# Differential attention: the join one tile later on VectorE, its ratio on GpSimd, both maxima of a tile in one instruction, both half turns in one step

## The reference

```python
def diff_attn_core(q, k, v, lam):
    s = jnp.einsum('bhiqd,bhikd->bhiqk', q, k).astype(jnp.float32) * (q.shape[-1] ** -0.5)
    p = jax.nn.softmax(s, axis=-1)
    a = (p[:, :, 0] - lam * p[:, :, 1]).astype(v.dtype)
    return jnp.einsum('bhqk,bhkd->bhqd', a, v)
```

## Time and profile before

| | |
|---|---|
| median of the runs | 1715.51 us (3 runs, 1715.05 to 1716.44) |
| the profiled execution | 1713.77 us, of which the span from first to last instruction 1712.0 us |
| PE busy | 1637.2 us, 96% |
| PEld busy | 1363.9 us, 80% |
| DVE busy | 890.8 us, 52% |
| ACT busy | 509.3 us, 30% |
| POOL busy | 624.5 us, 36% |
| mean granted clock of TensorE | 0.973 of full speed |

### The profile page before, as it was taken

How to read it: one execution, slowest core, us unless ns; L and a number is a source line. 1 busy time by engine, 2 the same in 40 slices (tenths; PEclk the granted TensorE clock), 3 DMA queues, 4 the chain that set the end, 5 groups by cost and what they waited for, 6 DMA issues and landing times.

```text
span 1712.0 us, 23461 instructions
## 1 busy us (share of the span) xinstructions
PE 1637.2 (96%) x9182; PEld 1363.9 (80%) x9182; DVE 890.8 (52%) x1168; ACT 509.3 (30%) x880; POOL 624.5 (36%) x349
## 2 busy tenths in 40 slices
PE   5899989998999999999999899999999899999997
PEld 2777878887888888888888788777857788888886
DVE  2500207627972772783685667309964753525263
ACT  3322326424211211111122311128853322222221
POOL 1522256324422332332332343334503544444441
PEclk7899999998999999999999899999999899999998
DMA  9364121320252242334233032200002233323221
GB/s 366 133 232 162 62 71 49 124 84 22 94 176 72 95 163 83 98 109 136 76 122 99 1 123 87 74 25 2 5 34 71 64 99 99 98 88 106 88 87 50
DMA packets 49473, 163.79 MB, mean 96 GB/s; under 512 B 6376, under 2 KB 6632, under 8 KB 45808
## 3 DMA queue, kind: packets, MB, share of 16 engines
q1 hardware_dynamic: 49392, 162.68, 28.5%
HBM read 159.77 MB, written 2.10 MB: 95 GB/s over the span
## 4 chain that ended last, share of the span: by engine, by line
PE 85%; DVE 6%; issue 2%; ACT 2%; POOL 2%; DMA 2%; SPq 0%; DVEq 0%; ACTq 0%; POOLq 0%
PE ps L1414 24%; PE ps L1415 24%; PE ps L1416 24%; PE ps L1811 2%; PE ps L1773 2%; PE ps L1800 1%; PE ps L1687 1%; POOL h_lo L543 1%; PE ps L1677 1%; PE ps L1565 1%; DVE mod_acc L1026 1%; PE ps L1715 1%; DMA xc<-ctx_dram 1%; DVE h_hi L1136 1%; ACT tmp_b L744 1%
## 5 line engine op out<-in xcount | busy, mean ns | idle before, releaser
L532 POOL TENSOR_TENSOR w_lo<-raw,w_hi 128x1024 fp32r<-128x1024 f32 x189 | 469.5, 2489 | 880.4 <-ACT w_hi L682 880.3
L1414 PE MATMUL ps<-h_lo,w_hi 128*128 128x512 f32 (+1 forms) x1152 | 413.3, 359 | 18.7 <-DVE h_lo L1139 13.8
L1415 PE MATMUL ps<-h_hi,w_lo 128*128 128x512 f32 (+1 forms) x1152 | 411.8, 357 | 0.0
L1416 PE MATMUL ps<-h_hi,w_hi 128*128 128x512 f32 (+1 forms) x1152 | 408.7, 355 | 0.0
L682 ACT ACTIVATE w_hi<-raw 128x1024 fp32r<-128x1024 f32 x189 | 199.3, 1057 | 419.0 <-PE ps L1416 398.6
L1414 PE MATMUL ps<-hid_lo,w_hi 128*128 128x512 f32 (+1 forms) x784 | 276.1, 352 | 0.7 <-DVE hid_lo L1163 0.7
L1415 PE MATMUL ps<-hid_hi,w_lo 128*128 128x512 f32 (+1 forms) x784 | 276.1, 352 | 0.0
L1416 PE MATMUL ps<-hid_hi,w_hi 128*128 128x512 f32 (+1 forms) x784 | 274.4, 350 | 0.0
L1414 PEld LDWEIGHTS ps<-h_lo,w_hi 128*128 128x128 f32 x1152 | 220.9, 192 | 61.7 <-issue 22.1
L1416 PEld LDWEIGHTS ps<-h_hi,w_hi 128*128 128x128 f32 x1152 | 220.2, 191 | 32.0
L1415 PEld LDWEIGHTS ps<-h_hi,w_lo 128*128 128x128 f32 x1152 | 221.1, 192 | 29.9
(11 more groups left out here) (202 smaller groups left out, 2170.6 us busy)
## 6 DMA issues: line engine op xcount, KB each, us to landing
raw<-units_dram SPq DMA_DIRECT2D x189, 512.0 KB, 3.7
mod_ring<-w_mod_dram SPq DMA_DIRECT2D x96, 256.0 KB, 3.2
mod_big<-w_mod_dram SPq DMA_DIRECT2D x16, 1024.0 KB, 8.7
mod_late<-w_mod_dram SPq DMA_DIRECT2D x8, 1024.0 KB, 6.1
xl<-x_dram SPq DMA_DIRECT2D x2, 2048.0 KB, 11.2
bias<-bias_dram SPq DMA_DIRECT2D x8, 384.0 KB, 3.7
xc<-ctx_dram SPq DMA_DIRECT2D x2, 1024.0 KB, 13.3
out_dram<-out_t SPq DMA_DIRECT2D x8, 256.0 KB, 2.9
```

The lines of the kernel that those rows point to most:

```text
L532: nc.gpsimd.tensor_tensor(w_lo[:, s], raw[:, s], w_hi[:, s].bitcast(F32), op=ALU.subtract).then_inc(lo_made, 1)
L1414: mm(out, a[0], b[1], start=start, stop=False)
L1415: mm(out, a[1], b[0], start=False, stop=False)
L1416: return mm(out, a[0], b[0], start=False, stop=stop)
```

## The change

- `least1(n)` becomes one reduction over both maps, with one count of `m1`; `exps` waits for n + 1 counts.
- `ratio(n)` is split. The reciprocal stays on DVE (`inverse1`, raising the new `inv1`); the multiplication with lambda and the first sum goes to POOL (`ratio`, raising the new `r1`).
- `combine(n)` waits for `r1` and is issued one tile later: DVE's round is now reciprocal of tile n, join of tile n-1, reduction of tile n+2.
- PE's round is now scores of tile n+2, first half turn of tile n-1, products, second half turn of tile n-1. The sums of squares of heads 0 to 5 stand in round N1, that of head 6 behind the loop.
- ACT's round is now half copy 1 of tile n-3, exponential 0 of tile n, half copy 0 of tile n-2, exponential 1 of tile n.
- POOL no longer makes the operands of a head in one go: casts in the round of its tile 3, key differences in that of tile 0, query differences in that of tile 1, each behind that round's ratio; the squares follow in even rounds.

The diff, with the declarations of the two semaphores and the unchanged inner lines left out:

```diff
+            def ratio(n):
+                pool.wait_ge(inv1, n + 1)
+                nc.gpsimd.tensor_scalar(stat[:, 28 + n % 3:29 + n % 3], stat[:, 32 + n % 3:33 + n % 3], lam_t[:, 4:5],
+                                        l_first[:, n:n + 1], ALU.mult, ALU.mult).then_inc(r1, 1)
...
-            for h in range(HEADS):
-                if h + 1 < HEADS:
-                    if h:
-                        pool.wait_ge(s1, 8 * h)
-                        keys_high1(h + 1)
-                    queries_high1(h + 1)
-                    keys_low1(h + 1)
-                    queries_low1(h + 1)
-                if h:
-                    out_square(2 * h - 2)
-                    out_square(2 * h - 1)
+            queries_high1(1)
+            for n in range(4 * HEADS):
+                ratio(n)
+                h = (n + 1) // 4 + 1
+                if h < HEADS:
+                    if n % 4 == 3:
+                        pool.wait_ge(s1, 8 * (h - 1))
+                        keys_high1(h)
+                        queries_high1(h)
+                    elif n % 4 == 0:
+                        keys_low1(h, 0)
+                        keys_low1(h, 1)
+                    elif n % 4 == 1:
+                        queries_low1(h, 0)
+                        queries_low1(h, 1)
+                if n >= 6 and n % 2 == 0:
+                    out_square(n // 2 - 3)
+            out_square(2 * HEADS - 3)
...
             def exps(n, i):
-                act.wait_ge(m1, 2 * n + 2)
+                act.wait_ge(m1, n + 1)
...
-                for i in range(2):
-                    if 2 <= n <= N1 + 1:
-                        turned1(n - 2, i)
-                    if n < N1:
-                        exps(n, i)
+                if 3 <= n <= N1 + 2:
+                    turned1(n - 3, 1)
+                if n < N1:
+                    exps(n, 0)
+                if 2 <= n <= N1 + 1:
+                    turned1(n - 2, 0)
+                if n < N1:
+                    exps(n, 1)
                 if n >= 5 and n % 2 == 1:
                     out_copy((n - 5) // 2)
-                if n == N1 + 1:
+                if n == N1 + 2:
...
             def least1(n):
-                for i in range(2):
-                    dve.wait_ge(s1, 2 * n + 2)
-                    c = 16 + 2 * (n % 2) + i
-                    V.tensor_reduce(stat[:, c:c + 1], scores_ps(n)[:, TOK * i:TOK * i + TOK], AX.X, ALU.min).then_inc(m1, 1)
-
-            def ratio(n):
+                dve.wait_ge(s1, 2 * n + 2)
+                c = 16 + 2 * (n % 2)
+                V.tensor_reduce(stat[:, c:c + 2], scores_ps(n).rearrange("p (i k) -> p i k", i=2), AX.X, ALU.min).then_inc(m1, 1)
+
+            def inverse1(n):
                 dve.wait_ge(e1, 2 * n + 2)
-                c, d = 22 + n % 3, 28 + 2 * (n % 3)
-                st.wait(V.reciprocal(stat[:, d:d + 1], stat[:, c:c + 1]))
-                st.wait(V.tensor_scalar(stat[:, d + 1:d + 2], stat[:, d:d + 1], lam_t[:, 4:5], l_first[:, n:n + 1],
-                                        ALU.mult, ALU.mult))
+                V.reciprocal(stat[:, 32 + n % 3:33 + n % 3], stat[:, 22 + n % 3:23 + n % 3]).then_inc(inv1, 1)
 
             def combine(n):
-                d = 29 + 2 * (n % 3)
+                dve.wait_ge(r1, n + 1)
+                d = 28 + n % 3
...
-            for n in range(N1):
-                ratio(n)
-                combine(n)
+            for n in range(N1 + 1):
+                if n < N1:
+                    inverse1(n)
+                if n:
+                    combine(n - 1)
                 if n + 2 < N1:
                     least1(n + 2)
...
                 if n + 2 < N1:
                     scores1(n + 2)
-                if n >= 1:
-                    turn1(n - 1, 1)
+                if n:
+                    turn1(n - 1, 0)
                 if n >= 3:
                     weigh1((n - 3) // 2, (n - 3) % 2)
-                if n == N1 - 1:
+                if n == N1:
                     pe.wait_ge(oneh_in, 32)
-                    for h in range(4):
+                    for h in range(HEADS - 2):
                         sub_sums(h)
-                if n == N1:
-                    for h in range(4, HEADS - 1):
-                        sub_sums(h)
-                if n < N1:
-                    turn1(n, 0)
+                if n:
+                    turn1(n - 1, 1)
+            sub_sums(HEADS - 2)
```

More of the change, by code:

```diff
@@ L328, in build @@
         first_in = sem("first_in")
+        inv1 = sem("inv1")
+        r1 = sem("r1")
         m1 = sem("m1")
@@ L628, in queries_high1, with keys_low1, queries_low1 @@
                 nc.gpsimd.tensor_copy(aqh[h % 2][:], q1[:, h]).then_inc(qh1, 1)
-            def keys_low1(h):
-                pool.wait_ge(kh1, h + 1)
-                for sl in (slice(0, 384), slice(384, TOK)):
-                    ins = nc.gpsimd.tensor_tensor(akl[h % 2][:, sl], k1[:, h, sl], akh[h % 2][:, sl].bitcast(F32),
-                                                  op=ALU.subtract)
-                ins.then_inc(kl1, 1)
-            def queries_low1(h):
-                pool.wait_ge(qh1, h + 1)
-                for sl in (slice(0, 256), slice(256, LAT)):
-                    ins = nc.gpsimd.tensor_tensor(aql[h % 2][:, sl], q1[:, h, sl], aqh[h % 2][:, sl].bitcast(F32),
-                                                  op=ALU.subtract)
-                ins.then_inc(ql1, 1)
+            def keys_low1(h, piece):
+                if piece == 0:
+                    pool.wait_ge(kh1, h + 1)
+                sl = slice(384 * piece, 384 * piece + 384)
+                ins = nc.gpsimd.tensor_tensor(akl[h % 2][:, sl], k1[:, h, sl], akh[h % 2][:, sl].bitcast(F32), op=ALU.subtract)
+                if piece:
+                    ins.then_inc(kl1, 1)
+            def queries_low1(h, piece):
+                if piece == 0:
+                    pool.wait_ge(qh1, h + 1)
+                sl = slice(256 * piece, 256 * piece + 256)
+                ins = nc.gpsimd.tensor_tensor(aql[h % 2][:, sl], q1[:, h, sl], aqh[h % 2][:, sl].bitcast(F32), op=ALU.subtract)
+                if piece:
+                    ins.then_inc(ql1, 1)
             def out_square(m):
@@ L653, in _ @@
             queries_high1(0)
-            keys_low1(0)
-            queries_low1(0)
+            for piece in range(2):
+                keys_low1(0, piece)
+            for piece in range(2):
+                queries_low1(0, piece)
             lows(FIRST["out1"] - 1, FIRST["out1"])
             pool.wait_ge(lo_made, FIRST["out1"] + AHEAD)
-            for h in range(HEADS):
-                if h + 1 < HEADS:
-                    if h:
-                        pool.wait_ge(s1, 8 * h)
-                        keys_high1(h + 1)
-                    queries_high1(h + 1)
-                    keys_low1(h + 1)
-                    queries_low1(h + 1)
-                if h:
-                    out_square(2 * h - 2)
-                    out_square(2 * h - 1)
+            queries_high1(1)
[16 more added lines that the diff above has]
+            out_square(2 * HEADS - 3)
             lows(FIRST["out1"], FIRST["mlp1"] - 1)
```

4 lines of the change are left out of this document (2 added, 2 removed).

## The result

The changed kernel takes 1716.74 us (median of 20 runs, 1713.74 to 1722.58); the kernel before, run beside it, 1713.30 us (20 runs, 1712.34 to 1716.65). The ratio is 1.0019, with a 95% interval of 1.0011 to 1.0027: 3.3 us slower, between 1.9 and 4.6. The forecast was 2.9 us more, and inside 0.2%. The size was right; the reasons for two thirds of it were. (The interval reaches to both sides of 0.2%, so that the trace, not the timing, has to carry the account.) The new order costs 1.6 to 1.7 us, at the two places named. The 1.0 us forecast for contention did not come, and what came instead, TensorE's granted clock, is nowhere in the prediction.

What follows compares the result with a forecast made beforehand. TensorE's chain, 3.35 us a tile, was taken as the bound, with VectorE in reserve. Start 0.6, end 1.3 and contention 1.0 made 2.9 us more: 1716.7 profiled, 1718.4 as median (1.74 above); range 1713.0 to 1722.8.

Steps and rivals of the forecast that it cites:

- the two places named: Start and end of the differential attention, where the new order was to cost 0.6 and 1.3 us.
- contention: Tiles 8 to 24 by four: GpSimd's keys' differences and square hold the next join beyond its reserve; 1.0 us more.
- What bounds the kernel: Differential attention: TensorE's chain sets 3.35 us a tile; VectorE is nearly full with a reserve, so relieving it gains 0.0.
- The start: First tiles of the attention: the first join stands behind a reduction; 0.6 us later, bounds 0 and 1.
- The end: Behind the last scores: TensorE idles 0.9 us more, plus 0.38 for moved turns; 1.3 us, bounds 0.8 and 1.8.
- e: The moment at which both exponentials of a tile are done; scores were to start at e + 0.15.
- The upper bound of 3.3 us: Contention's upper case: with a ratio of 0.61 us, the join loses 0.65 us five times.
- The order of starts: After the reciprocal, VectorE goes on in 0.04 us, GpSimd in 0.10, so the join goes ahead of the ratio.
- VectorE as the bound: First rival, attention: VectorE sets the pace, so 2.7 us less, 1712.8; chance 0.10.
- The join setting the pace: Second rival: the ratio gets ahead of the join on 27 tiles, 4 us on top, 1722.4; chance 0.20.
- GpSimd late: Third rival: queries' differences of the next head 0.4 us late, six times, 2.4 on top, near 1721; chance 0.10.
- A stall at the first use: Fourth rival: GpSimd's first use of a new operation stalls, delaying tile 4's scores; 3 us more, 1721.5; chance 0.05.

Runs made afterwards that it cites:

- e3: Changed kernel with one sum of squares moved into each of TensorE's three idle gaps behind the last scores: 1712.79 us, ratio 0.9994.
- e9: Changed kernel with the ratio back on VectorE and the join of tile n-1 ahead of reciprocal and ratio of tile n: 1714.22 us, ratio 1.0003.
- e7: Changed kernel with GpSimd's ratio issued three times, the first two into unused columns: 1718.77 us, ratio 1.0022.
- e2: Changed kernel with the ratio back on VectorE between reciprocal and join, GpSimd still waiting for the reciprocal: 1733.24 us, ratio 1.0121.
- e1: Kernel before with one part of the change alone, both maxima of a tile in one reduction: 1715.07 us, ratio 1.0011.
- e6: Changed kernel, unedited, run and traced a second time: 1719.87 us, ratio 1.0022.
- e12: Changed kernel, unedited, traced a third time: a single execution of 1716.57 us.
- e8: e4 with extra matmuls in the gaps at the start (5 and 3) and ahead of the last head's sum (5): 1713.76 us, ratio 0.9992.
- e4: Kernel before with three sums of squares moved into TensorE's gaps behind the last scores: 1710.95 us, ratio 0.9986.
- e10: Kernel before with sums in the gaps behind the last scores and both maxima in one instruction: 1712.46 us, ratio 0.9993.
- e5: Changed kernel with 14 extra matmuls of ones in TensorE's idle gaps at the start of the attention: 1716.41 us, ratio 1.0012.
- e11: e3 with the extra matmuls of e5 in the gaps at the start: 1712.05 us, ratio 0.9994.

## Why the prediction came out right, and where it was not

**What bounds the kernel: right.** TensorE's pitch went from 3.350 to 3.353 us while VectorE got 0.4 us of idle time a tile. That the new turns have a join to wait for did not matter, with a reserve of 0.22 us (forecast 0.13 to 0.2).

**The start: 0.6 forecast, 0.5 measured** (18.2 against 17.7 us to the scores of tile 6). Measured from the first scores, which came 0.34 us earlier in after, tile 4 was due at 1164.26 and came at 1164.13; tile 6 was due at 1170.91 and came at 1170.78. The chain named (reduction, join, turns, copy, exponential) is the one in the rows.

**The end: 1.3 forecast, 1.1 measured.** The idle times were 0.95, 0.95 and 0.67 us where 1.05, 1.05 and 0.6 were worked out: 0.8 us more than before, and 0.3 for the turns that had moved in. e3 took the holes away and got 2.33 us.

**Contention: 1.0 forecast, 0 measured.** GpSimd's sequence was right: the ratio ended 0.22 us behind the join (0.2 forecast), and the square at 1187.24 + 0.61 = 1187.85, 3.8 us after e = 1184.04 (3.9 forecast). Two sizes behind it were not. The join that began at 1187.51 had 0.34 us of that square ahead of it and took 0.17 longer, where 0.4 was charged; and the reserve was 0.22 us, not 0.15. So 0.17 fell inside the reserve on each of the five tiles, and TensorE has no idle time there. e9, without a ratio on GpSimd, has the same pitch. The upper bound of 3.3 us was a ratio of 0.61 alone; it is 0.35, and e7 shows that with 0.97 it is not the join that fails first.

**The order of starts: right, with the reason given.** The join started 0.08 us after the reciprocal, GpSimd 0.27; the 0.04 against 0.10 were both too small, their order was right. By the Trainium skill's page "SBUF — State Buffer", section "Who interferes with whom", a VectorE instruction with two SBUF inputs contends with a GpSimd instruction that reads SBUF, and the later one waits. The page makes no exception for a short one. The trace agrees, 1.03 us beside a join against 0.35 alone; here it is GpSimd that waits. e2 shows the other sign: joins of 1.28 to 1.69 us.

**The rivals.** VectorE as the bound: refuted by the pitch and by e1. The join setting the pace: not in after; e2 priced it, at 10.6 us in held joins and not 4, since casts, differences and squares and not one ratio get ahead. GpSimd late: not in after, by 0.63 us at tile 12 and 0.54 at tile 4 (1163.59 against 1164.13); shown in e7. A stall at the first use: refuted, the first ratio took 0.35 us at 1157.94, after idle time that ended with the reciprocal it waited for.

**What the prediction left out: the clock.** Its rows had the granted clock at 1.00 in the middle of the stage, and it never asked about the edges, where the change makes holes. The structural terms are 0.59 + 1.09 = 1.7 us; the measured difference is 3.3 (3.4 between the medians). Of after's 20 executions, the 14 up to 1719 us have a mean of 1715.79, the six above it 1721.24. The mean of before's 20, none of them above 1717, is 1714.15. Without its six, after is 1.64 us slower in the means, near the structural terms, but 2.6 in the medians (1715.92 against 1713.30), so the agreement can't be leaned on. What is clear is that after has long executions more often. Its 31, with e6 and e12, hold 12 above 1719; all 111 of before hold 6, and 8 above 1717.3, the same line less the 1.7. The line was drawn after the results were known. Nor is it settled that the order is the reason. e6, with 6 of 10, ran on another chip than e9, which shares the start and most of the end and had 1 of 10.

That the clock makes these executions long is shown in one trace, e6. The mean clock of whole executions points the same way, 0.9745 for the 14 and 0.9715 for the six, but one of the six, 1720.51 us, has 0.978, and the traced one of e3, with 10.2 us at half clock at the start, has 0.976: the mean over the span does not tell what one stage lost. That a sum without this term met the difference is in part luck: a term of 1.0 that was not there stood in for about 1.6 that the structural terms leave.

The absolute forecast was too high for another reason. 1718.4 stood on a median of before of 1715.51 from three runs, 1.74 above the profiled execution; in 20 runs the median is 1713.30, 0.47 below it. From there 2.9 us more are 1716.2, where 1716.74 was measured.

**Left open.** Why the half clock behind the sums of squares lasts 3.4 us in one execution and 20.5 in another, and why the new order meets the long ones more often. Traces show it in every kernel here; e8, with extra matmuls in the hole ahead of it, did not remove it. Nor did any run change the new start's order alone, so its 0.5 us is read from the trace. The fall of the clock at the start occurred in e3, e2 and e7 and in none of after, e6, e9 and e12, nor in any kernel with before's start (before, e1, e4, e10) or a held one (e5, e8, e11); that the emptier start allows it is a guess, which counts of this size don't show.

## What to carry to other kernels

Ask which engine's pitch moves when another one swings: VectorE, busy for 9.78 of 10 us, was not the bound, and freeing it by 12.6 us gave nothing. Where the bound is a full engine in the middle, the price of a new order lies at its two ends, where each added dependence stands open as a hole; fill those holes with work that otherwise stands behind them (e4, 1.95 us less in its trace, ratio 0.9986). When an operation is moved beside one that shares its path to memory, look at which of the two is released first and by how much, and at the granted clock wherever the change makes TensorE idle.

## What the runs showed of the hardware

- A one-column multiplication with two per-partition scalars takes GpSimd 0.35 us alone, 0.97 for three in a row, and 1.03 beside a VectorE join that began 0.19 us ahead of it. It waits the join out.
- One reduction of 128x1536 from PSUM takes 1.76 us, two of 128x768 together 1.81: the second start costs 0.05 us.
- Behind matmuls with one or seven stationary columns (the sums of squares, the spreads) the granted clock stood at 0.50 in every trace, for 3.4 to 20.5 us, though PE was busy for the whole of most of those windows; each matmul of 128x512 then comes 0.43 us after the last, not 0.24. Two executions of one kernel (after and e6) differed by 4.7 us in the part with it, and 0.45 us for each microsecond of it makes 4.6. That the few columns are the reason was not tested.
